# A two-layer hybrid encoder: the order of its mixers, norms and recurrent scan changed, and each expert unit loaded in two transfers

## What is computed

```python
p = x @ w_in + b_in                      # 23 tiles of 128 columns, split among four mixers
A = attention(q, k, v)                   # RMS-normed heads, 2-D rotary, softmax over 256
B = rwkv7(p_B)                           # token shift, decays, one delta-rule scan per direction
C = s5(u)                                # complex diagonal scans, GELU, GLU
D = mlstm(qk, v, i, f, o)                # conv, gates, running-max matrix memory
m = sum(sigmoid(x @ w_gate[br] + b_gate[br]) * (mix[br] @ w_branch[br]) for br in (A, B, C, D))
x = layer_norm(ALPHA * x + m @ w_out)
if layer == 0: y = (silu(x @ w1) * (x @ w3)) @ w2          # width 2816
else:          y = sum of the 2 best of 8 such experts     # width 3584 each
x = layer_norm(ALPHA * x + y)
```

## Time and profile before

| | |
|---|---|
| median of three runs | 2055.73 us |
| the profiled execution, whole | 2052.61 us |
| its span, first to last instruction | 2050.2 us |
| mean granted TensorE clock | 0.965 |
| DVE busy | 692.8 us (34%) |
| ACT busy | 325.6 us (16%) |
| POOL busy | 101.3 us (5%) |
| read from HBM | 468.68 MB |

### The profile page before, as it was taken

One profiled execution on the slowest core, in us unless ns is written; L12 is line 12 of the kernel. 1 busy time (PEld: TensorE's weight loads), 2 busy tenths in 40 slices (PEclk: granted clock), 3 DMA queues, 4 the chain that ended last, 5 costly groups with the idle time before them and its releaser, 6 DMA issues. The chain is left out here.

```text
span 2050.2 us, 65356 instructions
## 1 busy us (share of the span) xinstructions
PE 1903.7 (93%) x30112; PEld 1689.7 (82%) x30112; DVE 692.8 (34%) x1435; ACT 325.6 (16%) x745; POOL 101.3 (5%) x44
## 2 busy tenths in 40 slices
PE   8999788889999899978788899999999999999996
PEld 7777687657777677768664899999999999999995
DVE  7964472510211396356342211111111111111113
ACT  3232222010100323232120100000000000000001
POOL 4400000000100160000000000000000000000000
PEclk9999999899999999989979999999999999999998
DMA  7233211234444323321016599999999999999992
GB/s 288 101 103 123 83 43 43 74 121 154 154 153 143 123 103 124 119 87 43 2 66 252 207 396 400 398 398 400 393 415 392 403 400 395 402 404 401 400 400 82
DMA packets 54475, 470.98 MB, mean 230 GB/s; under 512 B 5184, under 2 KB 5456, under 8 KB 20336
## 3 DMA queue, kind: packets, MB, share of 16 engines
q1 hardware_dynamic: 37744, 292.04, 37.2%
q10 hardware_dynamic: 16272, 175.06, 21.0%
q0 software_dynamic: 368, 2.64, 0.3%
HBM read 468.68 MB, written 1.05 MB: 229 GB/s over the span
## 5 line engine op out<-in xcount | busy, mean ns | idle before, releaser
L1010 PE MATMUL bank<-arena,ring 128*64 128x88 f32 x8192 | 333.1, 239 | 0.0
L1010 PEld LDWEIGHTS bank<-arena,ring 128*64 128x64 f32 x8192 | 320.0, 137 | 0.0
L1010 PE MATMUL bank<-arena 128*64 128x88 f32 x6144 | 244.8, 239 | 0.6 <-DVE arena L1902 0.6
L1010 PEld LDWEIGHTS bank<-arena 128*64 128x64 f32 x6144 | 236.9, 137 | 1.2 <-issue 0.9
L771 PE MATMUL bank<-xT,ring 128*128 128x256 f32 x1024 | 229.4, 384 | 0.0
L1869 DVE TENSOR_TENSOR arena<-arena,bank 128x88 f32<-128x88 f32 x224 | 54.6, 244 | 514.3 <-ACT arena L1262 514.3
L771 PEld LDWEIGHTS bank<-xT,ring 128*128 128x128 f32 x1024 | 195.8, 192 | 32.4 <-issue 5.5
L1262 ACT ACTIVATE arena<-bank 128x88 f32<-128x88 f32 (+1 forms) x246 | 63.0, 256 | 921.6 <-PE bank L1010 726.6
L929 PE MATMUL bank<-arena,ring 128*64 128x88 f32 x4096 | 178.1, 239 | 0.2 <-issue 0.2
L929 PEld LDWEIGHTS bank<-arena,ring 128*64 128x64 f32 x4096 | 167.2, 137 | 4.7 <-issue 0.4
L450 PE MATMUL bank<-xT,ring 128*128 128x256 f32 x736 | 164.6, 386 | 3.2 <-DMA ring<-in_w_in 3.2
(11 more groups left out here) (418 smaller groups left out, 1791.4 us busy)
## 6 DMA issues: line engine op xcount, KB each, us to landing
ring<-in_moe SPq DMA_DIRECT2D x66, 1536.0 KB, 9.3
ring<-in_moe ACTq DMA_DIRECT2D x62, 1536.0 KB, 10.0
arena<-in_moe SPq DMA_DIRECT2D x49, 1536.0 KB, 9.6
arena<-in_moe ACTq DMA_DIRECT2D x47, 1536.0 KB, 9.4
ring<-in_ffn SPq DMA_DIRECT2D x22, 1536.0 KB, 6.5
ring<-in_w_gate SPq DMA_DIRECT2D x32, 1024.0 KB, 4.9
ring<-in_w_in SPq DMA_DIRECT2D x14, 1536.0 KB, 6.5
ring<-in_w_branch SPq DMA_DIRECT2D x8, 1024.0 KB, 4.8
```

The lines of the kernel that those rows point to most:

```text
L1010: last = mm(bank[c:c + STRIP, g * CAP:(g + 1) * CAP], w[:, at:at + STRIP], rhs[:, kt, :], start=(kt == 0), stop=(kt == KT - 1), skip_group ...
```

## The change

Mixers. `MERGE_UNITS` gets another order. Head means and rotations move from `attention` into `s5_end`, and on VectorE `scale_heads` and `rotate` into `s5`. `attention` keeps one gate, (2,3), behind its scores; branch 2 goes behind attention's output. Between token shift and features stand gates (0,0) to (0,2). VectorE does the shift before it copies attention's output. The token-major copies become 16 full transposes a layer, placed in levels 1 and 2, each bank read by ScalarE in four pieces. Levels 1 to 5 hold a gate each. The scan starts each bank with the parts that need no new state, and each chunk ends with a quarter of branch 0. Mean and variance go into `mlstm`, where three of the four gates of branch 3 stand between the heads and the last one behind them; VectorE does the first exponents before the end of rwkv. A bank may be filled in another order than opened (`filled_at`), and the arena places of mLSTM move.

Norms. Each half of the tokens has its own chain: statistics, Sqrt on ScalarE (its table loaded ahead by a dummy), reciprocal on VectorE, scaling. The last output unit is multiplied bank by bank, the dense layer tells when its first two banks are done, and the last norm folds gain and bias into two operations.

Expert units. SyncE and ScalarE issue two transfers for each unit: up weights (1 MB) when the slot's old unit has gone through `hidden`, down weights (0.5 MB) when it has gone through `down`. `down` waits for its own semaphore.

```diff
-MERGE_UNITS = [(2, 0), (2, 1), (2, 2), (2, 3), (2, 4), (0, 0), (0, 1), (0, 2), (0, 3), (0, 4), (1, 0), (1, 1), (3, 0),
-               (3, 1), (1, 2), (1, 3), (3, 2), (3, 3), (1, 4), (3, 4)]
+MERGE_UNITS = [(2, 0), (2, 1), (2, 2), (2, 3), (2, 4), (0, 0), (0, 1), (0, 2), (0, 3), (1, 0), (1, 1), (1, 2), (1, 3),
+               (0, 4), (3, 0), (1, 4), (3, 1), (3, 2), (3, 3), (3, 4)]
...
-        FILL_GATES = {1: (1, 2), 3: (1, 3)}
-        ROWS_LEVEL = 3
-        S5_BU_AT, S5_READ_AT, S5_ANGLE_AT = 1, {5: 0, 8: 1, 11: 2}, {1: 0, 3: 1, 6: 2, 9: 3}
+        FILL_GATES = {1: (0, 3), 2: (1, 0), 3: (1, 1), 4: (1, 2), 5: (1, 3)}
+        ROWS_LEVEL, TOKENS_LEVEL = 3, (1, 2)
...
-                branch(L, 2, range(2, 4))
-                for k in range(4):
-                    gate(L, 0, k)
+                gate(L, 2, 3)
...
             def rwkv(L):
-                branch(L, 0, range(4))
+                branch(L, 2, range(4))
...
+                pe.wait_ge(S["rw_sq"], L + 1)
+                b = open_bank(("rwss", L), "rw_ss")
+                fill(mm(b[:, :], C("sum64"), rw_gate2(), start=True, stop=True))
+                pe.wait_ge(S["rw_sg"], L + 1)
+                b = open_bank(("rwg", L), "rw_gate")
+                for q in range(2):
+                    last = mm(two(b)[:, q, :], M("g2", q * P, P), rw_sh[:, 7, :], start=True, stop=True)
+                fill(last)
+                gate(L, 0, 0)
+                pe.wait_ge(S["rw_bonus"], L + 1)
+                b = open_bank(("rwb", L), "dve_freed")
+                fill(mm(b[:, :], C("sum64"), rw_bonus_in(), start=True, stop=True))
+                gate(L, 0, 1)
+                gate(L, 0, 2)
                 pe.wait_ge(S["rw_feat"], L + 1)
...
                 for lev in range(6):
+                    if lev in TOKENS_LEVEL:
+                        k = TOKENS_LEVEL.index(lev)
+                        for dp in range(4):
+                            b = open_bank(("rwt", L, k, dp), "rw_tok")
+                            for cp in range(2):
+                                last = nc.tensor.transpose(b[:, cp * P:(cp + 1) * P],
+                                                           (rw_BT, rw_KT)[k][:, dp, cp * P:(cp + 1) * P], ident)
+                            fill(last)
                     if lev in FILL_GATES:
                         gate(L, *FILL_GATES[lev])
...
+                part(z, 0, MM(2), V, start=True)
                 for s in range(NCH):
-                    lanes = [(dp, (s if dp < 2 else NCH - 1 - s), h) for dp in range(4) for h in (0, 64)]
-                    rw_S = rw_S2[:, s % 2, :, :]
+                    state = lane(rw_S2[:, s % 2, :, :])
                     pe.wait_ge(S["rw_S"], NCH * L + s + 1)
-                    b = open_bank(("rwZ", L, s), "rw_Z")
-                    for dp, ch, h in lanes:
-                        o = b[h:h + 64, dp * 64:(dp + 1) * 64]
-                        mm(o, rw_AR[h:h + 64, dp, ch, 0, :], rw_S[h:h + 64, dp, :], start=True, stop=False)
...
+                    fill(part(z, s, AR(0), state, stop=True), ("rwZ", L, s))
+                    y = open_bank(("rwY", L, s), "rw_Y")
+                    part(y, s, state, AR(1), start=True)
+                    part(y, s, V, MM(3))
...
-                    for dp, ch, h in lanes:
-                        last = mm(b[h:h + 64, dp * 64:(dp + 1) * 64], rw_XT[h:h + 64, dp * 4 + ch, :],
-                                  rw_Z[h:h + 64, dp, :], start=True, stop=True)
-                    fill(last)
+                    fill(part(u, s, XT, lane(rw_Z), start=True, stop=True), ("rwU", L, s))
...
-                        b = open_bank(("rwS", L, s), "dve_freed")
...
+                    fill(part(y, s, lane(rw_U), MM(1), stop=True), ("rwY", L, s))
+                    if s < NCH - 1:
+                        z = open_bank(("rwZ", L, s + 1), "rw_Z")
+                        part(z, s + 1, MM(2), V, start=True)
+                    branch(L, 0, (s,))
+            def rwkv_mean(L):
                 pe.wait_ge(S["rw_Y"], NCH * (L + 1))
                 b = open_bank(("rwmu", L), "dve_freed")
...
                 gate(L, 2, 1)
                 s5_read(L, 3)
+                rotations(L)
                 gate(L, 2, 2)
                 pe.wait_ge(S["s5_g"], L + 1)
                 b = open_bank(("glu", L), "s5_glu")
@@ -701,7 +719,6 @@
                         last = mm(two(b)[:, q, :], M("glu", ct * W + q * P, P), s5_g[:, ct, :], start=(ct == 0),
                                   stop=(ct == 1))
                 fill(last)
-                gate(L, 2, 3)
             def ml_rows(L):
                 pe.wait_ge(S["ml_rows"], L + 1)
...
                 scores(0)
-                gate(L, 3, 3)
+                rwkv_variance(L)
+                scores(1)
+                gate(L, 3, 0)
                 pe.wait_ge(S["ml_v"], L + 1)
                 for h in range(4):
-                    if h < 3:
-                        scores(h + 1)
                     branch(L, 1, (h,))
                     reads(h)
+                    if h < 2:
+                        scores(h + 2)
+                        gate(L, 3, h + 1)
+                gate(L, 3, 3)
                 pe.wait_ge(S["ml_h"], 4 * (L + 1))
...
+                    order = [(c, k) for c in range(2) for k in range(4)]
+                    if u == 3:
+                        order = [(c, k) for k in range(4) for c in range(2)]
...
+                        if last_step and k == 1:
+                            last.then_inc(S["dn_half"], 1)
...
                     def down(s):
+                        pe.wait_ge(down_loaded[s], loads + 16)
...
-                    transposed_x(2, lambda tt: pe.wait_ge(S["ln_z2"], 4))
+                    assert len(jobs) % RB == 0
+                    transposed_x(2, lambda tt: pe.wait_ge(S["ln_z2"], 2 * tt + 2))
...
+                        for dp in range(4):
+                            b = bank_of(act, ("rwt", L, k, dp))
+                            for odd in (0, 64):
+                                for h in (0, 64):
+                                    ins = nc.scalar.copy((rw_Bt, rw_Kt)[k][h:h + 64, dp, odd // 64::2, :],
+                                                         b[odd:odd + 64, 0:T].rearrange("p (c t) -> p c t", c=2)[:, :, h:h + 64])
+                            step(ins, "rw_tok", hold=False)
...
             def norm(k, scale):
-                act.wait_ge(S["ln_sum"], TT * (k + 1))
-                step(f(ln_rstd, ln_mv[:, :, 1], ACT.Ln, scale=scale * scale, bias=EPSL))
-                step(f(ln_rstd, ln_rstd, ACT.Exp, scale=-0.5, bias=C("eps", 5 if scale == 0.5 else 6, 1)), "ln_rs")
+                f(small[:, 60:61], C("ones", 0, 1), ACT.Sqrt)
+                for tt in range(TT):
+                    act.wait_ge(S["ln_sum"], TT * k + tt + 1)
+                    step(f(ln_rstd[:, tt:tt + 1], ln_mv[:, tt, 1:2], ACT.Sqrt,
+                           bias=C("eps", 5, 1) if scale == 0.5 else EPSL), "ln_sd", hold=False)
...
-                products(L, 0, range(4))
+                attention_out(L)
...
+                products(L, 2, range(0, 2))
...
+                    products(L, 0, (s,))
...
+                exponents(0)
+                weights(0)
+                exponents(1)
+                rwkv_out(L)
                 for h in range(4):
-                    exponents(h)
+                    if h:
+                        weights(h)
+                        if h < 3:
+                            exponents(h + 1)
                     products(L, 1, (h,))
...
-                dve.wait_ge(S["ln_rs"], k + 1)
...
+                    if k == 3:
+                        dve.wait_ge(S["lnp_loaded"], 16)
                         for hf in range(2):
                             o = slice(hf * 512, (hf + 1) * 512)
-                            step(tt_(x_tok[:, tt, o], x_tok[:, tt, o], ln_gb[:, 0, o], ALU.mult))
-                            step(tt_(x_tok[:, tt, o], x_tok[:, tt, o], ln_gb[:, 1, o], ALU.add), "ln_done",
-                                 hold=False)
+                            step(stt(x_tok[:, tt, o], sums(tt, hf), ln_mv[:, tt, 0:1], ln_gb[:, 0, o], ALU.subtract,
+                                     ALU.mult), hold=hf == 1)
+                    dve.wait_ge(S["ln_sd"], TT * k + tt + 1)
+                    step(nc.vector.reciprocal(ln_rstd[:, tt:tt + 1], ln_rstd[:, tt:tt + 1]))
+                    for hf in range(2):
+                        o = slice(hf * 512, (hf + 1) * 512)
+                        if k == 3:
+                            step(stt(x_tok[:, tt, o], x_tok[:, tt, o], ln_rstd[:, tt:tt + 1], ln_gb[:, 1, o], ALU.mult,
+                                     ALU.add), "ln_done", hold=False)
+                        else:
...
             def expert_unit(steps, s, src):
+                m = s % EX_RING
+                sp.wait_ge(S["h_filled"], steps + (FF_STEPS + s - EX_RING + 1))
```

(3 more changed lines are left out.)

268 lines of the change are left out of this document (134 added, 134 removed).

## The result

The changed kernel takes 1962.73 us (median of four runs, 1959.36 to 1964.6), the kernel before 2054.68 us beside it: a ratio of 0.9546 with a 95% interval of 0.9519 to 0.9574, so 88 to 99 us less. In the profiled executions the span went from 2050.2 to 1962.2 us.

The account below looks back on a forecast made before the run. TensorE, busy 93% of the span, was taken to bound the kernel. From the profiled 2052.6 us, minus 70 (mixers), minus 16 (norms), plus 3 (expert wait) gave 1970; 3.1 us to the median made 1973 us, range 1945 to 2008.

Parts of the forecast that it names:

- The idle time left: Mixers: TensorE idle 20 us a layer after the change, from 42 and 43.5 us.
- The chain from the end of the shift to the features: Mixers before `rw_feat`: operations placed one after the other give 37 us, against 46.7 us before.
- one of my signs: Mixer levels 1 to 5: one gate each and no wait above 1 us.
- A branch quarter of 2 us covers the state update: Scan: a branch quarter behind each chunk covers the state update, leaving 2.7 us idle of 5.0.
- 2.7 us saved a layer: Token copies: sixteen full transposes at 1.91 us replace small matmuls, 128 of which take 4.6 us at full clock.
- Half of the loss regained: Mixers: half the time lost to TensorE's lower clock returns, 7.5 and 11.5 us in the two layers.
- The norms: Four norms: 4.6, 2.6, 4 and 4.5 us saved, together 16 us.
- The extra wait and the transfers: Expert loop: a fourth TensorE wait a unit costs 3 us in all; splitting the transfers costs 0.
- Rival 1: Expert loop: smaller transfers run at 350 GB/s and starve TensorE, 125 us more, 2098 us; chance 4%.
- Rival 2: Expert loop: DMA engines just miss at 389 GB/s, 28 us more, 2000 us; chance 12%.
- Rival 3: Mixers: feature chain stays 46.7 us and half of mLSTM's gain is lost, 12 us a layer, 1997 us; chance 10%.
- rival 4: Mixers: moved gates open other gaps, so only the norms gain, 2040 us; chance 2%.

Follow-up runs that it names:

- the moved gates: Changed kernel with the five gates of levels 1 to 5 all ahead of the wait for the features, none in the levels: 1982.4 us, ratio 0.9627.
- the columns' cut: Changed kernel with expert transfers cut by columns to 512 and 256 KB, rows of 4 and 2 KB, all 128 partitions: 1965.33 us, ratio 0.9569.
- the mixers alone: Changed kernel with the old norms and whole expert units, so only the mixer and scan edits against the kernel before: 1978.82 us, ratio 0.9619.
- three small edits: Changed kernel with whole units, second S5 read later, branch 2's products before the tanh wait, first head's read before branch 1: 1943.37 us, ratio 0.9435.

## Why the prediction was right, point by point

*The sum.* The time is 10 us below the forecast. Half of that is in the profiled execution, 1964.4 us against the sum of 1970: 4 us more from the mixers and 1 us less lost in the expert loop. The other half is the step to the median: I added 3.1 us, and this kernel's median lies 1.7 us under its profiled execution.

*The mixers.* Forecast 32 and 38 us, measured 32.8 and 41.2; alone 73 to 84 us with the projections. The idle time left was forecast at 20 us a layer and is 17.5 and 18.2. By parts, in layer 0, forecast and found: attention 2.9 and 0.2; features 6.5 and 6.4 (the bank 2 and 2.95, the features 3 and 2.8); levels 2.2 and 4.6; scan 2.7 and 1.8; mLSTM 5.3 and 4.5. The chain from the end of the shift to the features was placed at 37 us, operation by operation; it takes 191.65 - 152.99 = 38.7 us. So the method of placing the chain is good to a microsecond or two; what it missed are handovers: in the levels the bank before the first gate costs 1.57 us, not 0.7 (and so one of my signs, no wait above 1 us in levels 1 to 5, did not come), and two waits of 0.7 and 0.8 us for ScalarE's copies and for TensorE's own issue stand in levels 3 and 4.

*The scan* was right in its sum and wrong in its cause. The step "A branch quarter of 2 us covers the state update" gave the quarters a wait that is gone without them (0.19 us a step).

*The copies.* The step "2.7 us saved a layer" is mis-sized: it took 4.6 us for the 64 small matmuls from a row of 32 records, and in their new place they take 4.06. Their form is worth 1.0 us a layer: 1.9 us less work, of which a bank wait takes back 0.9. The remainder of the 6.45 us of the earlier trace rows, 2.4 us, belongs to their old place, behind the longest wait, at a low clock. That the mixers' sum came out all the same is in part luck: this term was too large, the idle time that went was 2.5 and 2.8 us more than forecast.

*The clock.* "Half of the loss regained" gave 7.5 and 11.5 us. Busy time fell by 8.2 and 14.9 us, 1.9 of it each for the copies: 6.3 and 13.0. Half was a choice and not worked out, and one execution can tell such sizes only to 7 us, so that they fit is in part luck. That clock is lost with idle time is borne out by the moved gates: 11 us more idle time, a mean granted clock of 0.975 to 0.979 against 0.982 to 0.984, and 17 to 20 us in the medians. How much a single wait costs in clock is not fixed: one of 2.0 us brought 0 to 3.5 us.

*The norms.* 16 forecast, 16.1 in the trace, 15 to 24 by themselves. The last norm was to take 9.2 us from the first statistic to the last addition; it runs from 1950.54 to 1959.71.

*The extra wait and the transfers.* I took 3 us for the wait and nothing for the transfers. Whole units leave the changed kernel's time alone; the split in the kernel before costs 2 to 8 us, which the changed kernel doesn't show; why the two differ stays open. Rival 1's ground, that smaller transfers run slower, does not hold for queued ones down to 256 KB at the rate of this loop. Its threshold, slower than before once the rate is below 366 GB/s, fits the runs: at 387 GB/s the time is 1989 us, at 348 it is 2084, and a line between them crosses 2055 at 360. The gain begins to shrink earlier, as soon as the rate is under the 399 GB/s of the steady part. The 849 us that rivals 1 and 2 give the loads stand in no row; they mean 402 GB/s, close to that 399. Rival 2 put a price of 28 us on 389 GB/s, and rows of 2 KB, with 387 GB/s, cost 26, though through ScalarE's held issues. Its evidence, however, was no guide: rate divided by busy share. It gave 350 GB/s for spaced loads; for rows of 2 KB it gives 387 / 1.05 = 369, though they ran at 387, and for the columns' cut 387, though that ran at 399. Only the back-to-back rate of 419 told what the loop can reach.

Rival 3 (the chain to the features stays at 46.7 us) and rival 4 are refuted by the features' wait and by the mixers alone.

## What to carry to other kernels

Give each wait of the bounding engine a filler of its own instead of a block of fillers in one place: five gates in front of one wait cost 17 to 20 us against one in each gap, 11 us of it idle time and the rest, as far as the granted clock tells, clock. Place the chain operation by operation before moving anything; it was right to 2 us in 38, and the waits it left were then worth another 19 us to three small edits. Split a transfer by columns and keep all 128 partitions; where the loop takes nearly all that the queues deliver, keep rows long (8 and 4 KB, and 4 and 2 KB, cost nothing here; 2 KB throughout cost 26 us). And look at who issues: when the queues fall behind, an engine that issues transfers between its other instructions is held at the issue.

## What the runs showed of the hardware that I had not expected

Transfers that write to 64 partitions each nearly halve the rate of the whole stream: 219 GB/s against 399, although both halves were always queued. Rows of 1 KB ran at 348 GB/s, of 2 KB at 387, of 8 KB at 419, which fits about 9 ns a row on top of its bytes, an estimate. A DMA issue on ScalarE takes about 0.35 us while the queues keep up and up to 6.4 us with rows of 2 KB, and ScalarE computes nothing meanwhile. The records of TensorE's semaphore waits in the loop take 51 ns each among its weight loads, and its period of 3.64 us is the same with three or four waits a unit. And the granted clock differs between executions of the same instructions: 0.94, 0.94 and 0.91 for layer 0's old mixers with nearly the same idle time (42.0, 42.0 and 40.5 us), 7.5 us of busy time, and the same 128 matmuls (L568) behind the same wait of 2.79 us take 8.69 us in the changed kernel and 7.20 in the one with the old copies.
